# Seven column groups instead of three in the modulation phase of a decoder block, in five k ranges

## The reference

```python
mod = silu(c) @ ada_w + ada_b                       # 2048 x 12288
sh1, sc1, g1, sh2, sc2, g2 = split(mod, 6)
u = rms_norm(x, mix_norm_pre) * (1 + sc1) + sh1     # 256 x 2048
proj = u @ w_in                                     # 2048 x 16384
rq, rk, rv, rg, mq, mk, mv, ga, gb = split(proj)
y_ret = (silu(rg) * group_norm(retention(rotary(rq), rotary(rk), rv))) @ ret_w_o
y_moba = causal_attention(mq, mk, mv) @ moba_w_o
y = (sigmoid(ga) * y_ret + sigmoid(gb) * y_moba) @ w_out
x = x + (1 + g1) * rms_norm(y, mix_norm_post)
u = rms_norm(x, ffn_norm_pre) * (1 + sc2) + sh2
a, b = split(causal_conv3(u @ ffn_w_up), 2)         # 2048 x 11264
x = x + (1 + g2) * rms_norm((silu(a) * b) @ ffn_w_down, ffn_norm_post)
```

## Time and profile before

| what | us |
|---|---|
| median of three runs (lowest, highest) | 1903.84 (1898.79, 1909.73) |
| the profiled execution | 1903.79 |
| its span in the trace | 1902.1 |
| mean granted clock of TensorE | 0.98 |

### The profile page before, as it was taken

How to read it: one execution, slowest core, us unless ns; L and a number is a source line. 1 busy time by engine, 2 the same in 40 slices (tenths; PEclk the granted TensorE clock), 3 DMA queues, 4 the chain that set the end, 5 groups by cost and what they waited for, 6 DMA issues and landing times.

```text
span 1902.1 us, 25236 instructions
## 1 busy us (share of the span) xinstructions
PE 1826.3 (96%) x8856; PEld 1537.0 (81%) x8856; DVE 1330.4 (70%) x1960; ACT 856.7 (45%) x984; POOL 100.9 (5%) x141
## 2 busy tenths in 40 slices
PE   3869999999999999999999988999999999999997
PEld 3658887888888888888888877888888888888886
DVE  6997877867676767678766666776667777754555
ACT  4214444444445445444444546444444444444443
POOL 0000111111111111111000000000000000000000
PEclk9879999999999999999999998999999999999999
DMA  9997777787778777788655653555555555555552
GB/s 354 360 353 261 242 256 265 240 270 256 253 248 280 248 263 251 265 280 289 242 181 188 229 177 124 187 183 192 177 193 181 186 189 178 193 191 190 198 195 92
DMA packets 247407, 432.63 MB, mean 227 GB/s; under 512 B 9413, under 2 KB 100213, under 8 KB 246705
## 3 DMA queue, kind: packets, MB, share of 16 engines
q1 hardware_dynamic: 227552, 360.77, 57.4%
q0 software_dynamic: 18688, 67.33, 9.4%
q10 hardware_dynamic: 1104, 3.70, 0.5%
HBM read 429.66 MB, written 2.10 MB: 227 GB/s over the span
## 4 chain that ended last, share of the span: by engine, by line
PE 88%; DVE 6%; DMA 3%; issue 2%; ACT 1%; SPq 0%; DVEq 0%; POOLq 0%; ACTq 0%
PE ps L703 17%; PE ps L429 15%; PE ps L431 15%; PE ps L430 15%; PE ps L705 9%; PE ps L742 4%; PE ps L744 4%; PE ps L743 4%; DVE ada_acc L1164 3%; DMA ada_ring<-in_ada_w 2%; DMA ada_first<-in_ada_w 1%; PE ps L451 1%; DVE w_low L1091 1%; DVE ada_acc L1117 1%; PE ps L483 1%
## 5 line engine op out<-in xcount | busy, mean ns | idle before, releaser
L762 ACT ACTIVATE w_high<-stage 128x1024 fp32r<-128x1024 f32 x616 | 651.1, 1061 | 888.1 <-PE ps L431 497.5
L1091 DVE TENSOR_TENSOR w_low<-stage,w_high 128x1024 fp32r<-128x1024 f32 x616 | 751.9, 1222 | 357.1 <-ACT w_high L762 356.2
L429 PE MATMUL ps<-w_high,lhs 128*128 128x512 f32 x1408 | 560.7, 398 | 12.1 <-DVE lhs L1128 10.8
L431 PE MATMUL ps<-w_high,lhs 128*128 128x512 f32 x1408 | 552.7, 393 | 0.0
L430 PE MATMUL ps<-w_low,lhs 128*128 128x512 f32 x1408 | 552.4, 392 | 0.0
L703 PE MATMUL ps<-lhs,w_high 128*128 128x512 f32 x1408 | 500.3, 400 | 2.2 <-issue 2.2
L705 PE MATMUL ps<-lhs,w_low 128*128 128x256 f32 x1408 | 396.4, 282 | 0.0
L1117 DVE SCALAR_TENSOR_TENSOR ada_acc<-ada_ring,c_act,ada_acc 128x256 f32<-128x256 f32 x480 | 230.7, 481 | 137.3 <-DMA ada_ring<-in_ada_w 133.8
L429 PEld LDWEIGHTS ps<-w_high,lhs 128*128 128x128 f32 x1408 | 267.5, 190 | 67.4 <-DVE lhs L1128 11.1
L703 PEld LDWEIGHTS ps<-lhs,w_high 128*128 128x128 f32 x1408 | 265.7, 189 | 68.7 <-issue 2.5
L431 PEld LDWEIGHTS ps<-w_high,lhs 128*128 128x128 f32 x1408 | 266.8, 189 | 57.0
(11 more groups left out here) (168 smaller groups left out, 765.0 us busy)
## 6 DMA issues: line engine op xcount, KB each, us to landing
stage<-in_w_in SPq DMA_DIRECT2D x128, 1024.0 KB, 6.2
stage<-in_ffn_w_up SPq DMA_DIRECT2D x176, 512.0 KB, 4.3
ada_ring<-in_ada_w POOLq DMA_DIRECT2D x128, 512.0 KB, 6.4
stage<-in_ffn_w_down SPq DMA_DIRECT2D x44, 1024.0 KB, 5.0
ada_first<-in_ada_w SPq DMA_DIRECT2D x32, 1024.0 KB, 12.5
stage<-in_ret_w_o SPq DMA_DIRECT2D x16, 1024.0 KB, 5.2
stage<-in_moba_w_o SPq DMA_DIRECT2D x16, 1024.0 KB, 4.9
stage<-in_w_out SPq DMA_DIRECT2D x16, 1024.0 KB, 5.0
```

Source lines behind the costliest of these rows:

```text
L429: pe.matmul(acc, hi, w_high[:, slot, k, :], start=kt == 0, stop=False)
L431: last = pe.matmul(acc, lo, w_high[:, slot, k, :], start=False, stop=kt == KT - 1)
L762: act.activation(w_high[:, h % 4, :, :], stage[:, slot, 2 * (h % 2):2 * (h % 2) + 2, :], ACT.Copy).then_inc(high_ready, 1)
L1091: dve.tensor_tensor(w_low[:, h % 4, :, :], stage[:, slot, 2 * (h % 2):2 * (h % 2) + 2, :], w_high[:, h % 4, :, :].bitcast(F32), ALU.subtra ...
```

## The change

Four things are changed.

**First phase.** Seven groups are worked in it: RV, RQ, RK as before (their sums stay in PSUM) and the four groups of gate b ("streamed"). For a streamed group one k range is summed in bank 6 (token tile 0) and bank 7 (token tile 1); the result goes to `gate_b` in SBUF, by a copy on ACT in the first range (L985) and by an add on DVE in the others (L1369). The five k ranges hold 2, 4, 4, 4 and 2 k tiles, that is 7, 14, 14, 14 and 7 halves, 56 in all. The sums of shift and scale for one range are made together, by 16 instructions of 512 columns (the outer ranges) or of 1024 (the inner ones), on one accumulator; for the next range they stand between the halves of the present one. `u` is computed on ACT instead of DVE. `x` is loaded first. The loads of the weights are in halves of 0.5 MB on eight semaphores.

**Later groups.** The MoBA sets hold GA where they held GB; the four separate groups for a gate fall away. There are still 44 groups. The sigmoid of gate b is two instructions in group 7. The chunks of the other modulation parts run beside groups 7 to 38 instead of 3 to 34; what splits `lhs` for `ret_w_o` has moved into the last MoBA group.

**Up product.** For each k tile the four products with `w_high` come first, then the four with `w_low`.

**Tail.** The last down step does the first two k tiles for all columns, then the last two by token tile: token tile 0 is finished, squared and normed while PE works token tile 1. The final scaling is in two instructions of 1024 columns per token tile, with two stores.

The core of the diff (tables and bookkeeping left out):

```diff
-G_FIRST = 3
-FIRST_COLS = (COL_RV, COL_RQ, COL_RK)
-FIRST_BANKS = (2, 0, 4)
+G_FIRST = 7
+FIRST_COLS = (COL_GB, COL_GB + NC, COL_GB + 2 * NC, COL_GB + 3 * NC, COL_RV, COL_RQ, COL_RK)
+FIRST_BANKS = (6, 6, 6, 6, 2, 0, 4)
+FIRST_PAIRS = ((0,), (1, 2), (3, 4), (5, 6), (7,))
+FIRST_ORDER = ((0, RV0, 1, RQ0, 2, RK0, 3),) + ((0, 1, RV0, 2, 3, RQ0, RK0),) * (STAGES - 2) + ((0, RV0, 1, RQ0, 2, RK0, 3),)
+SUM_BEHIND = (RK0,) + (RQ0,) * (STAGES - 2) + (None,)
...
@@ sync
-            for kb in range(KT // KB):
-                first_chunk(kb, 0, 2 * kb)
...
+            for t in range(T):
+                sp.dma_start(x_sb[:, t, :], x[0, t * P:(t + 1) * P, :]).then_inc(x_in[t], 16)
+            for slot in range(2):
+                first_ada(0, slot)
+            n = 0
+            for st in range(STAGES):
+                for g in FIRST_ORDER[st]:
+                    for pair in FIRST_PAIRS[st]:
+                        first_load(n, st, pair, g)
...
+                        st_, ops = ada_ops_behind(n)
+                        for i in ops:
+                            if i % ada_rows(st_) == 0:
+                                first_ada(st_, i // ada_rows(st_))
+                        n += 1
...
-                for g, col in enumerate((COL_MQ, COL_MK, COL_MV, COL_GB)):
+                for g, col in enumerate((COL_MQ, COL_MK, COL_MV, COL_GA)):
...
@@ tensor
+            def first_streamed(n, st, j, summed):
+                for t in range(T):
+                    n_out(4 * st + j - 1, t)
+                    if t == 1:
+                        pe.wait_ge(ada1_cols, 2 * summed)
+                    for i, pair in enumerate(FIRST_PAIRS[st]):
+                        if t == 0:
+                            pe.wait_ge(lhs_ready, pair + 1)
+                            pe.wait_ge(split_ready, n + i + 1)
...
+                        if t == 1:
+                            last.then_inc(used, 1)
+                    if t == 0:
+                        last.then_inc(n_first, 1)
...
+            for st in range(STAGES):
+                summed = st + 1
+                for g in FIRST_ORDER[st]:
+                    if g < 4:
+                        first_streamed(n, st, g, summed)
+                        behind = 4 * st + g
+                    else:
+                        first_resident(n, st, g)
+                    n += len(FIRST_PAIRS[st])
+                    if g == SUM_BEHIND[st]:
+                        sum_first(st + 1, behind)
+                        summed += 1
...
                         for ct in range(4):
                             pe.matmul(ps[:, 4 * parity + ct, :], w_high[:, h % 4, k, ct * P:(ct + 1) * P], lhs[:, kt, :],
                                       start=kt == 0, stop=False)
+                        for ct in range(4):
                             last = pe.matmul(ps[:, 4 * parity + ct, 0:SEQ], w_low[:, h % 4, k, ct * P:(ct + 1) * P],
                                              lhs[:, kt, 0:SEQ], start=False, stop=kt == KT - 1)
...
+            for t in range(T):
+                for n in range(4):
+                    if t == 0:
+                        pe.wait_ge(split_ready, 8 * (G_DOWN + DOWNS - 1) + 4 + n + 1)
+                    last_part(n, t, n, 1, True).then_inc(y2_done, 1)
...
@@ scalar
+            def first_u(st):
+                act.wait_ge(scale1_ready, st + 1)
+                for pair in FIRST_PAIRS[st]:
+                    for kt in (2 * pair, 2 * pair + 1):
+                        act.activation(src_b[:, kt, :], src_a[:, kt, :], ACT.Identity, bias=shift1[:, kt:kt + 1],
+                                       scale=scale1[:, kt:kt + 1]).then_inc(u_ready, 1)
+                    act.wait_ge(u_ready, 2 * pair + 2)
+                    lhs_pair(0, pair, src_b, -1)
...
@@ vector
+            for n in range(8 * G_FIRST):
+                st = prepares_before(n)
+                if st is not None:
+                    first_shift_scale(st)
+                    for pair in FIRST_PAIRS[st]:
+                        lhs_pair(0, pair, src_b)
+                add_streamed(n)
+                low_part(n, n // 2 % 4, n)
+                st, ops = ada_ops_behind(n)
+                for i in ops:
+                    first_ada(st, i)
```

466 lines of the change are left out of this document (284 added, 182 removed).

## The result

| | before | after |
|---|---|---|
| median of the runs on one chip, us | 1905.64 (1897.19 to 1911.07) | 1893.85 (1890.62 to 1898.47) |
| span of the profiled execution, us | 1902.1 | 1892.2 |

The ratio of the times is 0.9932, with a 95% interval of 0.9918 to 0.9947. The change makes the kernel 12 us faster, not 33 us: the time lies 3 us above the prediction's range.

The account below looks back on a forecast made before the run. PE was taken to bound the kernel except in the first phase, which is VectorE's with the loads close behind. 64 + 1.3 + 1 - 89 - 8 - 2.5 = -33.2 from 1903.8 gives 1871 us; range 1853 to 1891.

Parts of the forecast that it names:

- Four groups fewer: Behind the first phase: four groups at 22.26 us each fall away, -89.0 us; the other 37 stay as they were.
- Later groups: Chunks beside groups 35 to 38 and lhs halves in the last MoBA group: together +1 us, bounds 0 and 6.
- First phase: Seven groups in the first phase: it ends at 225 us instead of 161, +64 us.
- group 7: First group after the first phase, limited by DVE already before: two adds come in, +1.3 us.
- the chain between ranges: First phase, between k ranges: PE's sums 1.8, shift and scale 0.6, u and lhs 3.7, last low part 0.7: 6.9 us.
- Up: Up product, four short products in a row, then four long: 1.394 or 1.376 us instead of 1.408, -8 us (-5 or -11).
- Tail: After the last product only one token tile is left to norm, scale and store: 8.2 instead of 10.6 us, -2.5 us.
- The loads hidden: First phase: 65 MB of loads take 169 us at 384 GB/s or 190 at 342, under 225, so hidden.
- Lockstep: Rival, 12%: in the first phase DVE and PE wait for each other, clock falls; phase ends near 245, kernel takes 1891.
- Better overlap: Rival, 13%: DVE's chain is partly filled, the first phase ends at 212; with -11 in the up product, 1855.
- The slower up product: Rival, 5%: weight loads cannot lie under short products, 1.67 against 1.408 us, +92 us; the kernel takes 1971.
- the phase at 250: Case, 5%: late sums make streamed groups cost 22.3 us each; first phase ends at 161 + 89, kernel takes 1904 - 9.

## Why the prediction was wrong, step by step

*What bounds the kernel.* Right: the first phase is VectorE's (18.5 us came of halving its sums), and outside it the time is products times spacing. Incomplete: a second place, beside the late groups, was taken for TensorE's alone.

*Four groups fewer, -89.0.* Right on a ring that keeps up: from the first rotation product to the last result of `ret_w_o` before took 795.7 us with the ring of four, and after 708.1, 87.5 less, with the prediction's +1 for the later groups in it.

*Later groups, +1 with bounds 0 and 6: the step that failed most.* It measured about 12 us between the two traces. I set VectorE's 21 to 24 us of work a group against TensorE's 22 to 23 and let the lead absorb the rest. The working counted busy time only. VectorE's queue also holds waits, 167 us of them for the ring in the trace of before; the prediction does not name them and so put them at nothing. In before, with some 17 us of work a group (94.7 in 125 us), TensorE had no gap between 855 and 980 us. In after VectorE's work and these waits (15 in 125 us, 1.7 us on average) fill all of its time, and TensorE stands for 6.4 us. The price was in the trace of before: 5.5 us of sums against 0.75 us of issue and 6.4 of landing. Loading the last chunks not at all gave 9.4 us and loading them by four places 9.2, and on a ring of four +1 holds to within 1 us up to the last `ret_w_o` result. Two things stay open. The kernel before pays 2.5 to 8.5 us for its ring, by the execution, so how much of the 12 is the change's own is known to some 6 us only. And I had looked for the loss beside groups 35 to 38, while most of it is there by the end of group 35.

*First phase, +64 and group 7, +1.3: measured +73.3, 8.0 more. The second step that failed: the chain between ranges was priced too low.* The marks were 34.6 for the first product and 62.4, 108, 154.8 and 197.2 for the ends of the sums; they came at 36.2, 64.6, 113.3, 163.3 and 208.1. The single prices held: a sum of 1024 columns 1.28 alone and 1.20 from start to start (1.17), low half 1.14 (1.13), add 0.60 (0.60). What failed:
- *The chain between ranges, 6.9.* It measured 8.6, 8.6 and 8.3: 5 us in all. I halved the 3.56 us of the earlier trace rows because "x16" looked like sixteen sums. Each of these sums stands as two records, so the 3.56 us are eight sums, and there are eight again (3.54).
- *The start*, 1.6 us late (36.2 to 34.6). VectorE waited 3.4 us for the first `w_high` ahead of shift and scale.
- *Gaps inside the ranges.* 0.6 us in the first range and 1.0 to 1.5 in each inner one. Part of it are waits for ScalarE's `w_high` behind the chain, 1.13 us at 79.2 and 0.45 and 1.06 at 126.5 and 130.6: the chain does not end with the low part that I took for its end. In the fourth range I expected TensorE to be later than VectorE; there too TensorE waited 1.4 us for the last sum.
- The end: from 208.1 on it took 3 us less than I had allowed, 2 of them the allowance for late adds, which fell inside the ranges instead.

*Up, -8 (-5 to -11).* Right in sign, too large: -3.4. By the count the set of four and four is 1.399, and the stage is 3.4 us shorter. Of the two prices I had, 1.394 from spacings was nearly right, and 1.376 from gaps of turn-about products was not; I took the middle. The short one in a row is 0.12 as priced, the long one 0.2325 and not 0.2275. In a kernel's time the edit alone is not to be seen.

*Tail, -2.5.* Right: -2.7.

*The loads hidden, 0.* Right for the first phase as far as the kernel with half-wide sums shows: VectorE waits 0.8 us in it for the modulation's loads, though from 73 to 113 us their share is 1.05.

*The rivals.* Lockstep gave 1891, 3 us from the time, for a reason that the trace does not bear out. It had a third of the products at the lower clock in the inner ranges; these ran at 0.99, and the clock was down at 0.50 to 0.62 only in the 8 or 9 us between ranges. That the time lies near it is luck. Better overlap said a phase 51 us longer (its end at 212 against 161; halfway between 194 and 225 would have been 209.5). The kernel with moved sums comes near it: its first rotation product is 58.2 us later than before's (216.5 against 158.3). The change's own order, at 73.3, does not. The slower up product did not come, nor the phase at 250. Behind the former stood a sentence of the Trainium skill's page TensorE: Matmul & The Clock Gate (Part 3, The mechanism). The same section also lets a weight load into the background weight buffer be pulled ahead of running products, and the trace of after agrees with that: short products in a row start 0.12 us apart beside load records of 190 ns.

*The range* took in the ends of the known terms. Its own bounds do not add up to the 1861 to 1886 that it gives but to 1862 to 1891. What it lacked was a price for VectorE's waits once its idle time is used up; the bounds of 0 and 6 for the late groups came from a lead, not from a row.

## What to carry to other kernels

- A wait in slack is a debt. When work is added to an engine, add the waits in its queue to its busy time, and compare the sum with the pace of the engine that sets the time. The condition that the two rings here bear out is: landing plus issue is less than the time in which the places still full are used up (0.75 + 6.7 against 5.5 us failed, 0.75 + 5.4 against 8.2 held).
- Where a producer's last sum, TensorE's short sums and the next operands form a chain between stages, put independent work of the waiting engine into the chain, and move the window of work as a whole. Ending early by packing the work tighter (four halves, 1881.7) lost what moving it (two halves, 1868.7) won.
- Look at what one record is before halving a duration by its count.

## What was not expected of the hardware

- The same eight one-column sums took 3.3 to 3.54 us when TensorE had waited 3.5 us or more, and 1.84 when it came straight from products. The granted clock of the stretch was 0.50 and 1.00. Four of them behind a wait of 1.4 us took 1.02. A chain that empties TensorE pays here for the gap, for sums at half the clock and for products 0.43 us apart behind it: 13 at 117 us in after, 9 at 167.
- A ring load of 512 KB landed after 6.7 us and one of 256 KB after 5.4: half the size took a fifth less. By the sum above the shorter landing alone would not have been enough (6.15 against 5.5 us), and the longer time alone would (7.45 against 8.2); no run takes the two apart.
- With the two-slot ring the kernel before spread over 18 us (1893.9 to 1912.5 in 17 runs), after with the ring of four over 4 us (1881.5 to 1885.6 in 5 runs). That the ring makes the spread is not shown, and two kernels speak against it: before with the ring of four still spread over 10.6 us, at two levels (four runs at 1891.3 to 1893.6, eight at 1900.5 to 1901.8), and the shifted sums on the ring of two only over 3 us (1878.9 to 1881.7 in 6 runs). What makes it stays open.
